# Where layer 0's output product lets the modulation tiles run: the last eight weight tiles without any, the first twenty-four with more

## The chip, the cores and the metric

The kernel runs on one core of one Trainium2 chip. The metric is the time of one execution on the device in microseconds (us). A core has the engines PE (TensorE, matmuls), DVE (VectorE), ACT (ScalarE), POOL (GpSimd) and SP (SyncE, which here issues nearly all loads). Each takes its instructions strictly in its own order and waits on semaphores for the others.

## The reference, cut to what matters

Two pairs of transformer layers on a sequence of 256 tokens with 2048 channels, float32. The first pair (layers 0 and 1) is modulated: three vectors per layer come from one product of the 2048-element condition with a 2048 x 6144 matrix.

```python
def first_block(x, c, positions, w_ada, b_ada, w_in, ..., w_out, ln_g, ln_b):
    c_act = jax.nn.silu(c)
    for l in range(DEPTH):                       # DEPTH = 2
        mod = c_act @ w_ada[l] + b_ada[l]
        shift, scale, gate = jnp.split(mod, 3, axis=-1)
        h = _layernorm(x) * (1.0 + scale[:, None, :]) + shift[:, None, :]
        p = h @ w_in[l]
        ...
        y = jnp.concatenate([y_f, y_a], axis=-1) @ w_out[l]
        x = _layernorm(DEEPNORM_ALPHA * x + gate[:, None, :] * y, ln_g[l], ln_b[l])
    return x
```

The second pair (`even_layer`, `odd_layer`) is of the same kind without modulation. Nothing that is computed changes here; layer 1's shift and scale only have to be there when layer 1 begins.

## The kernel before, in words

Every instruction comes from one plan (`Plan.whole`). It first writes a list of jobs, one for each tile of weights (128 partitions x 1024 numbers, 512 KB), and `run` then walks this list and appends steps to an order that all engines follow, each taking its own part.

A **weight tile** (job mode `split`) goes through five stations: SP loads it into one of nine staging buffers `stg` (line 1406), ACT writes its rounded high part into one of four buffers `whi` (line 1893), DVE writes the rest into `wlo` (line 2214), PE multiplies three times with high and low parts of the activations (`Hh`, `Hl`; line 1506), and the end of PE's work frees the staging buffer. A **modulation tile** (mode `ada`) needs PE only at the very end: SP loads it into one of the same nine buffers, and DVE multiplies it with the condition and adds it into the accumulator `AC` (line 2127, the first of sixteen is a plain product on line 2223). That frees the buffer. Buffers are handed out strictly in the order in which the plan frees them.

`run` prepares a weight tile (load, ACT part, DVE part) three weight tiles ahead of its matmuls (`AHEAD = 3`). A modulation tile puts its DVE instruction in at the place where it stands in the list.

Layer 0's output product (`w_out(0, "w_out0")`) has 32 weight tiles: four groups of eight, a group for each 512 output columns. I call them t0 to t31. Each takes 12 matmuls of 512 columns. After a group DVE runs the "out" block: six instructions on 128x512 (lines 2377, 2127, 2382, twice) that apply the gate, add to X and take statistics. At the head of the product two things of the previous stage are late: the last gate of y (four instructions on line 2127, `Z` and `TMP`) and the split of y into `Hh` and `Hl` (`y_split`, line 2368: four pieces for t2 to t5, then two for t6 and t7). The order of these around the tiles is fixed by the plan, and every one of them stands in DVE's single row.

When t31 is done the layer's closing part follows (`post_norm`, a chain on DVE, PE and ACT), then layer 1 begins with `lead`.

`interleave(n0, extra, n1, some)` takes the list's jobs from `n0` on (the body, here 84 weight tiles: 52 of layer 0's other products, then the 32 of `w_out0`) and deals the modulation tiles (`extra`, 98 jobs) in between: 76 of them evenly beside the first `n1` = 52, the other 22 evenly beside the rest.

Of the kernel before, what the change touches and what calls it, by code (L numbers as in the profile page):

```python
# [61 lines left out]
class Plan:  # L62
# [991 lines left out]

    def interleave(self, n0, extra, n1, some):
        body = self.jobs[n0:]
        del self.jobs[n0:]
        out, e = [], 0  # L1060
        for i, j in enumerate(body):
            due = some * (i + 1) / n1 if i < n1 else some + (len(extra) - some) * (i + 1 - n1) / (len(body) - n1)
            while e < len(extra) and e < due:
                out.append(extra[e])
                e += 1
            out.append(j)
        out += extra[e:]
        self.jobs.extend(out)

    def lead(self, first, trans, layer, columns=None):  # L1070

# [24 lines left out]
    def whole(self):  # L1096
        self.banks.get()
        self.banks.put(0, ("ca", 1))
        begin0 = self.mla(0)
        first, rest = self.jobs[0:24], self.jobs[24:]  # L1100
        del self.jobs[:]
        self.ln(("x_landed", 32))
        self.normed(range(4))
        ada = [self.ada_pe(q) for q in range(8)]

        def setup_bias():
            b, fr = self.banks.get()
            self.step("bias", bank=b, free=fr)
            self.banks.put(b, self.tick("bias"))

        def table(kind, out, by=1):
            b, fr = self.now(self.banks)
            self.step(kind, bank=b, free=fr)
            self.banks.put(b, self.tick(out, by))

        def turn(n):
            self.step("turn", n=n)
            if n == 1:
                self.ar = (("scr_landed", 32), ("rope_tab", 2))
                begin0()  # L1120

        tables = [lambda: table("gains", "vec"), lambda: table("biases", "buckets", 2), lambda: table("angles", "angle"),
                  lambda: turn(0), lambda: turn(1)]
        self.jobs.extend(ada[0][0])

        def cols(q):
            ada[q][1]()

        def enter(q):
            self.mod_h(0, (q,))  # L1130
            if q == 7:
                self.zw = self.h[KT - 1]

        def enter0():
            cols(0)
            enter(0)

        def pair(q, n):
            if q < 8:
                self.jobs.extend(ada[q][0][2 * n:2 * n + 2])  # L1140

        self.jobs[4]["pre"] = setup_bias
        self.jobs[6]["pre"] = enter0
        for q in range(8):
            j0, j1, j2 = (first[8 * g + q] for g in range(3))
            j0["last_chunk"] = q == 7
            self.jobs.append(j0)
            if q == 0:
                pair(1, 0)
                pair(1, 1)  # L1150
                self.jobs.append(j1)
                pair(1, 2)
                pair(1, 3)
                self.jobs.append(j2)
                j2["after"] = lambda: cols(1)
                self.jobs.append(ada[2][0][0])
                ada[2][0][0]["pre"] = lambda: enter(1)
                self.jobs.append(ada[2][0][1])
                pair(2, 1)
                continue  # L1160
            pair(q + 1, 2)
            pair(q + 1, 3)
            self.jobs.append(j1)
            if q < 7:
                j1["after"] = lambda q=q: cols(q + 1)
                if q < 6:
                    ada[q + 2][0][0]["pre"] = lambda q=q: enter(q + 1)
                else:
                    j2["pre"] = lambda: enter(7)
            pair(q + 2, 0)  # L1170
            self.jobs.append(j2)
            if q < 6:
                j2["after"] = tables[q - 1]
            pair(q + 2, 1)

        n0 = len(self.jobs)
        self.jobs.extend(rest)
        self.w_out(0, "w_out0")
        ex = []
        for c0 in (2 * D, 2 * D + 1024):  # L1180
            ex += self.ada(0, c0, 1024)
        for c0 in (0, 1024, D, D + 1024):
            ex += self.ada(1, c0, 1024)
        self.interleave(n0, ex, 52, 76)

        def norm1():
            p = self.post_norm(0)
            self.ln(p["out"][1], p)

        def scale():  # L1190
            for fin in self.scale_sums:
                fin()

        n1 = self.lead(norm1, lambda qs: self.mod_h(1, qs), lambda: self.mla(1), scale)
        self.w_out(1, "w_out1")
        ex = []
        for c0 in (2 * D, 2 * D + 1024):
            ex += self.ada(1, c0, 1024)
        self.interleave(n1 + 6, ex, 70, 32)

        def norm2():
            p = self.post_norm(1)
            self.rms(p["squared"], p["ss"], 8)

        self.lead(norm2, lambda qs: self.transposed("en", None, qs), self.even)
        self.w_out(2, "even_w_out")

        def norm3():
            self.ar = (self.mm_last,)
            self.h_free = self.mm_last  # L1210
            self.rms(self.x[1, 3], None, 8)

        self.lead(norm3, lambda qs: self.transposed("on", None, qs), self.odd)
        self.w_out(3, "odd_w_out")
        self.run()
        self.drain()
        return self
# [36 lines left out]
def build(nc, A):  # L1254
    with ExitStack() as ctx:
# [28 lines left out]
        for whole, tiles in ((AR, stg), (ARL, wlo)):  # L1284
            tiles += [whole[:, 3072 + i * 1024:4096 + i * 1024].rearrange("p (k n) -> p k n", k=2) for i in range(EXTRA)]
# [98 lines left out]
        def sync(e):  # L1384
            q = Queue(e)
            e.dma_start(ROWS[0:16, :], A["c"].rearrange("a (k p) -> (a k) p", p=128)).then_inc(SEM["c_landed"], 16)
            e.dma_start(IDN[:, :], cst[:, 0:128]).then_inc(SEM["c_landed"], 16)
            for t in range(2):
                e.dma_start(X[:, t, :], A["x"][0, t * 128:(t + 1) * 128, :]).then_inc(SEM["x_landed"], 16)
            for kind, s in plan.order:  # L1390
                if kind == "load":
                    slot = s["slot"]
                    q.wait_all(s["free"])
                    w, rows, n = tile_shape(s["src"])
                    whole = stg[slot][:, :, :].rearrange("p k n -> p (k n)")
                    if w == "b_ada":
                        (_, _, _, l, c0), = s["src"]
                        e.dma_start(whole[0:1, :], A["b_ada"][l:l + 1, c0:c0 + n]).then_inc(SEM[f"landed{slot}"], 16)
                        continue
                    if rows * n == 1024:  # L1400
                        dst, pat = whole, [[1024, 128], [1, 1024]]
                    else:
                        dst, pat = stg[slot][:, :, 0:n], [[rows * n, 128], [n, rows], [1, n]]
                    src = bass.AP(A[w].tensor, tile_at[w], pat)
                    tile_at[w] += 128 * rows * n
                    e.dma_start(dst, src).then_inc(SEM[f"landed{slot}"], 16)
                elif kind == "out" and s["l"] == 3 and s["g"] == 3:
                    t = s["t"]
                    q.wait_ge(s["done"])
                    e.dma_start(A["out"][0, t * 128:(t + 1) * 128, 1536:2048], X[:, t, 1536:2048]).then_inc(SEM["out_last"], 16)  # L1410
            q.wait_ge(("out_landed", 96))
            q.wait_ge(("out_last", 32))
            q.wait_ge(("scr_landed", 32))
# [1301 lines left out]
```

## Time and profile before

| | us |
|---|---|
| median of 3 runs | 1558.52 |
| lowest and highest of them | 1557.95, 1561.76 |
| the profiled execution | 1556.26 |
| its span | 1554.4 |
| what lies around the span | 1.86 |
| PE busy in the span | 1486.9 |
| DVE busy in the span | 1065.7 |

The page gives PE as busy for 96% of the span and DVE for 69%. These are shares over the whole execution, of stages with different limits. The output product of layer 0 lies between 345 and 433 us of the span, and only that stretch and its surroundings are touched by the change. In the views below a start is given in us from the span's start; "idle before" in square brackets is the time for which the engine stood before this instruction, and who released it. An instruction on DVE is reported longer than the distance to the next start, since neighbours overlap by a little: distances between starts are what DVE's row costs.

### The profile page before, as it was taken

The numbers are of one execution on the slowest core, as the hardware profiler recorded it, in microseconds if no ns is written. First come the engines' busy times: TensorE is split into PE (matmuls) and PEld (weight loads), VectorE is DVE, ScalarE is ACT, GpSimd is POOL, SyncE is SP. The second block draws the span as 40 slices with busy tenths as digits, with TensorE's granted clock in tenths as the row PEclk, the third lists the DMA queues.
The fourth block names the chain that finished last, engine by engine and source line by source line (L and its number), as shares of the span: only waits on it lengthen the run. The fifth ranks groups of instructions, "written<-read, shape, count | busy, mean of one in ns | idle before, by whom it ended". The sixth has DMA issues, their size and how long they took to land.

```text
span 1554.4 us, 25460 instructions
## 1 busy us (share of the span) xinstructions
PE 1486.9 (96%) x10123; PEld 1316.1 (85%) x10123; DVE 1065.7 (69%) x1732; ACT 706.8 (45%) x1218; POOL 45.3 (3%) x66
## 2 busy tenths in 40 slices
PE   5999999989979999999979999999998999999999
PEld 3778789988869788998859997799987998889987
DVE  3348689899987667577575684875655667775653
ACT  2235234344345445444335444654444546665442
POOL 3000000000000000000000000010000000000000
PEclk9999999999989999999999999999999999999999
DMA  9999889998837556776745555466665554445673
GB/s 357 406 406 330 283 294 364 348 365 338 329 90 266 191 195 207 251 247 205 217 148 179 177 169 151 123 219 187 184 196 163 151 162 121 124 123 160 183 223 98
DMA packets 102126, 347.15 MB, mean 223 GB/s; under 512 B 11392, under 2 KB 21876, under 8 KB 101240
## 3 DMA queue, kind: packets, MB, share of 16 engines
q1 hardware_dynamic: 96888, 327.42, 62.7%
q0 software_dynamic: 5120, 18.11, 3.5%
q8 instruction: 80, 1.31, 0.3%
q14 instruction: 38, 0.31, 0.1%
HBM read 343.27 MB, written 2.21 MB: 222 GB/s over the span
## 4 chain that ended last, share of the span: by engine, by line
PE 78%; DVE 11%; issue 4%; DMA 4%; ACT 3%; SPq 0%; DVEq 0%; ACTq 0%
PE PM L1506 66%; PE PB L1506 8%; DVE wlo L2214 2%; DMA stg<-in_w_in 2%; DVE AC L2127 2%; ACT whi L1893 1%; DVE X L2127 1%; DMA stg<-in_w_ada 1%; ACT AR L1893 1%; PE PB L1741 1%; PE PB L1713 1%; PE PB L1816 1%; DVE SM L2127 0%; PE PB L1788 0%; ACT Hh L1893 0%
## 5 line engine op out<-in xcount | busy, mean ns | idle before, releaser
L2214 DVE TENSOR_TENSOR wlo<-stg,whi 128x1024 fp32r<-128x1024 f32 (+2 forms) x417 | 497.9, 1203 | 324.5 <-ACT whi L1893 322.2
L1893 ACT ACTIVATE whi<-stg 128x1024 fp32r<-128x1024 f32 (+2 forms) x417 | 430.3, 1038 | 455.2 <-PE PM L1506 348.5
L1506 PE MATMUL PM<-Hh,whi 128*128 128x256 f32 x1824 | 526.2, 291 | 11.5 <-DVE wlo L2214 7.6
L1506 PE MATMUL PM<-Hh,wlo 128*128 128x256 f32 x1776 | 500.3, 285 | 0.0
L1506 PE MATMUL PM<-Hl,whi 128*128 128x256 f32 x1824 | 497.7, 284 | 0.0
L1506 PEld LDWEIGHTS PM<-Hh,whi 128*128 128x128 f32 x1824 | 352.4, 193 | 29.5 <-issue 17.0
L1506 PEld LDWEIGHTS PM<-Hh,wlo 128*128 128x128 f32 x1776 | 343.6, 193 | 0.0
L1506 PEld LDWEIGHTS PM<-Hl,whi 128*128 128x128 f32 x1824 | 342.5, 193 | 0.4
L1506 PE MATMUL PM<-whi,Hh 128*128 128x512 f32 (+1 forms) x576 | 223.3, 389 | 0.4 <-DVE wlo L2214 0.4
L1506 PE MATMUL PM<-wlo,Hh 128*128 128x512 f32 (+1 forms) x576 | 220.1, 383 | 0.0
L1506 PE MATMUL PM<-whi,Hl 128*128 128x512 f32 (+1 forms) x576 | 218.3, 384 | 0.0
L2127 DVE SCALAR_TENSOR_TENSOR AC<-stg,CA,AC 128x1024 f32<-128x1024 f32 x120 | 153.6, 1280 | 6.6 <-DMA stg<-in_w_ada 4.0
L1506 PEld LDWEIGHTS PM<-whi,Hh 128*128 128x128 f32 x576 | 108.3, 188 | 23.4 <-issue 1.5
L1506 PEld LDWEIGHTS PM<-wlo,Hh 128*128 128x128 f32 x576 | 108.3, 188 | 21.0 <-issue 0.2
L1506 PEld LDWEIGHTS PM<-whi,Hl 128*128 128x128 f32 x576 | 107.1, 188 | 21.4
L1506 PE MATMUL PM<-whi,ARL 128*128 128x512 f32 (+1 forms) x272 | 86.1, 383 | 0.0
L1893 ACT ACTIVATE AR<-PB 128x384 f32<-128x384 f32 (+2 forms) x110 | 47.3, 471 | 75.4 <-PE PB L1506 28.0
L1506 PE MATMUL PB<-AR 64*128 64x256 f32 (+4 forms) x576 | 71.1, 353 | 3.5 <-ACT AR L1893 2.2
L1506 PEld LDWEIGHTS PB<-AR 64*128 64x128 f32 (+2 forms) x576 | 46.2, 170 | 21.2 <-issue 6.0
L1506 PEld LDWEIGHTS PM<-whi,ARL 128*128 128x128 f32 x272 | 51.1, 188 | 10.3 <-issue 0.4
L1506 PE MATMUL PM<-wlo,ARL 128*128 128x512 f32 (+1 forms) x144 | 54.4, 378 | 0.0
L1893 ACT ACTIVATE AR<-PM 128x256 f32<-128x256 f32 (+2 forms) x58 | 24.1, 466 | 57.1 <-PE PM L1506 57.1
(287 smaller groups left out, 1389.5 us busy)
## 6 DMA issues: line engine op xcount, KB each, us to landing
stg<-in_w_ada SPq DMA_DIRECT2D x163, 512.0 KB, 6.2
stg<-in_w_in SPq DMA_DIRECT2D x105, 512.0 KB, 5.4
stg<-in_even_w_in SPq DMA_DIRECT2D x80, 512.0 KB, 3.6
stg<-in_odd_w_in SPq DMA_DIRECT2D x72, 512.0 KB, 3.6
stg<-in_w_out SPq DMA_DIRECT2D x64, 512.0 KB, 4.5
stg<-in_even_w_out SPq DMA_DIRECT2D x32, 512.0 KB, 3.6
stg<-in_odd_w_out SPq DMA_DIRECT2D x32, 512.0 KB, 3.5
AR<-in_w_ada SPq DMA_DIRECT2D x29, 512.0 KB, 14.5
```

Source lines behind the costliest of these rows:

```text
L1506: return e.matmul(out, l, r, start=start, stop=stop, skip_group_check=True)
L1713: ins = e.transpose(B[:, kk * S + t * 128:kk * S + t * 128 + 128], XN[:, t, k * 128:(k + 1) * 128], IDN[:, :])
L1741: ins = e.matmul(B[:, 0:S], ar(UU + t * 1024 + s["g"] * 128, 128), CSS[:, t, :], start=t == 0, stop=t == 1)
L1816: ins = e.transpose(B[:, n * 128:(n + 1) * 128], L[:, n * 128:(n + 1) * 128], IDN[:, :])
L1893: return e.activation(out, x, f, **k)
L2127: return e.scalar_tensor_tensor(out=out, in0=in0, scalar=scalar, in1=in1, op0=op0, op1=op1)
L2214: e.tensor_tensor(wlo[s["slot"]][:, :, 0:n], stg[s["slot"]][:, :, 0:n], whi[s["hi"]][:, :, 0:n].bitcast(F32), ALU.subtract).then_inc(SEM[" ...
```

## The change

`interleave` gets a fifth argument, `bare`: the number of weight tiles at the body's end that get no extra job beside them. The call for layer 0 passes 8.

```diff
-    def interleave(self, n0, extra, n1, some):
-        body = self.jobs[n0:]
+    def interleave(self, n0, extra, n1, some, bare=0):
+        end = len(self.jobs) - bare
+        body, last = self.jobs[n0:end], self.jobs[end:]
         del self.jobs[n0:]
         out, e = [], 0
         for i, j in enumerate(body):
...
         out += extra[e:]
-        self.jobs.extend(out)
+        self.jobs.extend(out + last)
...
-        self.interleave(n0, ex, 52, 76)
+        self.interleave(n0, ex, 52, 76, 8)
```

The first 52 weight tiles keep their 76 jobs, since `n1` and `some` are the same. The last 22 modulation tiles, which stood beside 32 weight tiles, now stand beside 24. PE's, ACT's and POOL's orders of instructions are the same as before; DVE's and SP's are not. In the rows below every line number of the kernel after is one higher, because one line was added.

DVE, from the four pieces of `Hl` for t2 to t5 on. `AC<-stg` is a modulation tile, `wlo<-stg` the low part of a weight tile (here t3 to t6), `TMP<-TMP,PM` and `Z` the last gate. Before:

```order
L2368 TENSOR_TENSOR Hl<-Z,Hh 128x512 x4
L2214 TENSOR_TENSOR wlo4<-stg4,whi3 128x1024
L2127 SCALAR_TENSOR_TENSOR AC<-stg0,CA,AC 128x1024
L2214 TENSOR_TENSOR wlo5<-stg5,whi0 128x1024
L2127 SCALAR_TENSOR_TENSOR AC<-stg1,CA,AC 128x1024
L2214 TENSOR_TENSOR wlo7<-stg7,whi1 128x1024
L2214 TENSOR_TENSOR wlo3<-stg3,whi2 128x1024
L2127 SCALAR_TENSOR_TENSOR TMP0<-TMP0,PM0 128x512
L2127 SCALAR_TENSOR_TENSOR Z<-TMP0,Z 128x512
```

The same place after the change:

```order
L2369 TENSOR_TENSOR Hl<-Z,Hh 128x512 x4
L2128 SCALAR_TENSOR_TENSOR AC<-stg4,CA,AC 128x1024
L2215 TENSOR_TENSOR wlo0<-stg0,whi3 128x1024
L2128 SCALAR_TENSOR_TENSOR AC<-stg5,CA,AC 128x1024
L2215 TENSOR_TENSOR wlo1<-stg1,whi0 128x1024
L2128 SCALAR_TENSOR_TENSOR AC<-stg7,CA,AC 128x1024
L2215 TENSOR_TENSOR wlo3<-stg3,whi1 128x1024
L2224 TENSOR_SCALAR AC<-stg4,CA 128x1024
L2215 TENSOR_TENSOR wlo2<-stg2,whi2 128x1024
L2128 SCALAR_TENSOR_TENSOR TMP0<-TMP0,PM0 128x512
L2128 SCALAR_TENSOR_TENSOR Z<-TMP0,Z 128x512
```

The last gate now has four modulation tiles ahead of it since `Hl` x4, where it had two.

DVE from the first "out" block on (its last row is the one on `STA`). Before, the weight tiles are t11 to t15:

```order
L2382 BN_STATS STA<-X 128x6
L2127 SCALAR_TENSOR_TENSOR AC<-stg5,CA,AC 128x1024
L2214 TENSOR_TENSOR wlo6<-stg6,whi3 128x1024
L2214 TENSOR_TENSOR wlo7<-stg7,whi0 128x1024
L2127 SCALAR_TENSOR_TENSOR AC<-stg3,CA,AC 128x1024
L2214 TENSOR_TENSOR wlo4<-stg4,whi1 128x1024
L2127 SCALAR_TENSOR_TENSOR AC<-stg0,CA,AC 128x1024
L2214 TENSOR_TENSOR wlo5<-stg5,whi2 128x1024
L2214 TENSOR_TENSOR wlo1<-stg1,whi3 128x1024
```

After the change:

```order
L2383 BN_STATS STA<-X 128x6
L2215 TENSOR_TENSOR wlo7<-stg7,whi3 128x1024
L2128 SCALAR_TENSOR_TENSOR AC<-stg3,CA,AC 128x1024
L2215 TENSOR_TENSOR wlo4<-stg4,whi0 128x1024
L2128 SCALAR_TENSOR_TENSOR AC<-stg2,CA,AC 128x1024
L2215 TENSOR_TENSOR wlo5<-stg5,whi1 128x1024
L2128 SCALAR_TENSOR_TENSOR AC<-stg6,CA,AC 128x1024
L2215 TENSOR_TENSOR wlo8<-stg8,whi2 128x1024
L2128 SCALAR_TENSOR_TENSOR AC<-stg3,CA,AC 128x1024
```

Modulation and weight tiles now alternate strictly: to the second "out" block they are seven beside eight, where they were six beside eight.

DVE from the last modulation tile to the next "out" block, after the change (t22 to t26):

```order
L2128 SCALAR_TENSOR_TENSOR AC<-stg2,CA,AC 128x1024
L2215 TENSOR_TENSOR wlo1<-stg1,whi2 128x1024
L2215 TENSOR_TENSOR wlo6<-stg6,whi3 128x1024
L2215 TENSOR_TENSOR wlo7<-stg7,whi0 128x1024
L2215 TENSOR_TENSOR wlo3<-stg3,whi1 128x1024
L2215 TENSOR_TENSOR wlo4<-stg4,whi2 128x1024
L2378 TENSOR_TENSOR TMP0<-PM2,GT 128x512
L2128 SCALAR_TENSOR_TENSOR X<-X,TMP0 128x512
```

From t22 to t31 there is nothing on DVE but weight tiles and the "out" blocks; six modulation tiles stood there before.

## Rows read from the trace of the kernel before

**Rows 1.** The page's first line, and busy time by engine.

```profile
span 1554.4 us, 25460 instructions
PE 1486.9 (96%) x10123; PEld 1316.1 (85%) x10123; DVE 1065.7 (69%) x1732; ACT 706.8 (45%) x1218; POOL 45.3 (3%) x66
```

**Rows 2.** Busy time by stretch: columns in the second line.

```profile
core 0: us, PE busy (x) PEld busy (x) DVE busy (x) ACT busy (x) POOL busy (x), PEclk, DMA share, GB/s
333.00:345.00 12.00, 12.00 (x103) 12.00 (x101) 11.34 (x10) 5.24 (x5) 0.00 (x0) 1.00 1.02 411
345.00:375.50 30.50, 30.13 (x134) 24.59 (x132) 30.05 (x35) 16.51 (x20) 0.00 (x0) 1.00 0.87 326
375.50:411.00 35.50, 35.46 (x156) 29.40 (x157) 33.29 (x31) 13.81 (x13) 0.00 (x0) 1.00 0.92 357
411.00:433.00 22.00, 21.95 (x97) 17.84 (x95) 17.94 (x21) 7.43 (x7) 0.00 (x0) 1.00 0.78 286
455.00:475.00 20.00, 18.55 (x155) 18.37 (x155) 16.66 (x23) 14.10 (x21) 0.00 (x0) 0.99 0.44 130
```

**Rows 3.** Waits of 345 to 433 us: waiter, releaser, us, times, longest.

```profile
DVE wlo L2214 <- ACT whi L1893: 4.6, 5, 1.5
PE PM L1506 <- DVE wlo L2214: 0.4, 1, 0.4
```

**Rows 4.** The chain that ended last, between 373 and 434 us: start, us, what.

```profile
374.35 1.15 DVE wlo L2214
...
375.54 57.43 PE PM L1506 x252
...
432.99 0.70 DVE TMP L2377
```

**Rows 5.** DVE in order of time, from t3's low part to t11's.

```profile
350.40 1.22 DVE L2214 TENSOR_TENSOR wlo<-stg,whi 128x1024 fp32r<-128x1024 f32 x1
351.54 1.28 DVE L2127 SCALAR_TENSOR_TENSOR AC<-stg,CA,AC 128x1024 f32<-128x1024 f32 x1
352.73 1.22 DVE L2214 TENSOR_TENSOR wlo<-stg,whi 128x1024 fp32r<-128x1024 f32 x1
...
359.99 1.47 DVE L2368 TENSOR_TENSOR Hl<-Z,Hh 128x512 fp32r<-128x512 f32 x2
...
363.71 0.75 DVE L2223 TENSOR_SCALAR AC<-stg,CA 128x1024 f32<-128x1024 f32 x1
364.38 2.36 DVE L2214 TENSOR_TENSOR wlo<-stg,whi 128x1024 fp32r<-128x1024 f32 x2
...
374.27 2.35 DVE L2214 TENSOR_TENSOR wlo<-stg,whi 128x1024 fp32r<-128x1024 f32 x2
```

**Rows 6.** DVE further on: low parts of t16, t17, t18 and t19.

```profile
384.01 1.23 DVE L2214 TENSOR_TENSOR wlo<-stg,whi 128x1024 fp32r<-128x1024 f32 x1 [0.40 <-ACT whi L1893]
...
386.54 1.23 DVE L2214 TENSOR_TENSOR wlo<-stg,whi 128x1024 fp32r<-128x1024 f32 x1
...
389.10 1.23 DVE L2214 TENSOR_TENSOR wlo<-stg,whi 128x1024 fp32r<-128x1024 f32 x1
...
394.35 1.21 DVE L2214 TENSOR_TENSOR wlo<-stg,whi 128x1024 fp32r<-128x1024 f32 x1
```

**Rows 7.** PE in order of time: the first matmul of t0 and of t2.

```profile
345.00 0.40 PE L1506 MATMUL PM<-whi,ARL 128*128 128x512 f32 x1
...
350.46 0.39 PE L1506 MATMUL PM<-whi,Hh 128*128 128x512 f32 x1
```

**Rows 8.** PE after two waits, one long and one short.

```profile
329.01 0.40 PE L1506 MATMUL PM<-Hh,whi 128*128 128x256 f32 x1 [3.52 <-DVE wlo L2214]
...
332.76 0.28 PE L1506 MATMUL PM<-Hh,whi 128*128 128x256 f32 x1
332.88 0.28 PE L1506 MATMUL PM<-Hl,whi 128*128 128x256 f32 x1
...
462.25 0.63 PE L1713 MATMUL PB<-IDN,Z 128*128 128x128 f32 x4 [1.46 <-DVE Z L2333]
```

## The prediction, made before the changed kernel had run

> **What bounds the kernel now.** Three views in this order. The page first [rows 1]: PE is busy for 96% of the span, so the default is that only what makes PE wait or stop waiting counts, and DVE's 69% seems to leave room. Next the stretches [rows 2], because that 69% is an average. In layer 0's output product DVE is busy for 30.05 of 30.5 us, then 33.29 of 35.5, and only in the last third 17.94 of 22.0; the DMA engines run at 0.87, 0.92 and 0.78 of their time. PE is busy nearly throughout. So for two thirds of this stage PE, DVE and DMA are close to a tie, and the slack of DVE lies in the last third, exactly where the change removes work from it. Third, who waits for whom: over the whole product PE waits once, 0.4 us for a low part [rows 3]. The chain shows where: DVE's low part of t11, and from then 252 matmuls (21 tiles) in 57.43 us without a break until t31 ends at 432.97, when the closing part starts at once [rows 4]. After 375.54 the stage is PE's alone.
>
> **PE's pace and DVE's price list.** 57.43 / 21 is 2.73 us for a tile. t0 begins at 345.00 and t2 at 350.46 [rows 7], the same 2.73. So PE reaches t6 at 350.46 + 4 x 2.73 = 361.4, t11 at 375.54, and t19 at 375.54 + 8 x 2.73 = 397.4. On DVE, distances between starts [rows 5]: a low part 351.54 - 350.40 = 1.14 us, a modulation tile 352.73 - 351.54 = 1.19 (1.2 below), the plain product that opens an accumulator 364.38 - 363.71 = 0.67.
>
> **What the change removes.** Six modulation tiles leave the ten last weight tiles, some 6 x 1.2 = 7.2 us of DVE time. Their place from t22 on is beside PE work that does not wait [rows 3, 4], so I cost the removal at nothing: what hides them is the unbroken run of matmuls. It would be worth something only if PE waited there, and the closing part starts with PE's last matmul in either order.
>
> **What it adds.** The same instructions, earlier. Since DVE runs without a gap from 350.40 to beyond 382, each one put ahead of a needed result makes it later by its full price. DVE's order up to `Hl` x4 is unchanged, so 350.40, where that ends, is a fixed point [rows 5]. Three results decide:
>
> - The last `Hl` pieces, for t6 and t7. Before them now stand three modulation tiles and the plain product, where two tiles stood: + 1.2 + 0.67 = 1.9 us. The first piece began at 359.99 [rows 5] and takes 0.7 (1.47 for the two), so it ends at 362.6 instead of 360.7. PE arrives at 361.4: PE waits 1.2 us. t7's low part, two more places back, adds 0.4.
> - t11. By then seven modulation tiles and the plain product have run, where it was five: + 2.4 us. t11's low part was ready at 375.49 and PE took it at 375.54 [rows 4]; it now starts at 377.9. PE is late by 2.4 in total, of which the first item is part, not an addition.
> - t19, the first tile behind the second "out" block. Counted from 350.40, fifteen modulation tiles against ten: + 5 x 1.2 = 6.0 us. Its low part ended at 394.35 + 1.21 = 395.56 [rows 6], so now 401.6; PE would be there at 397.4. Late by 4.2 us in total.
>
> From t22 on DVE has only 1.14 us of work for a tile besides the "out" blocks, against PE's 2.73, so nothing later is late: what is lost by t19 stays lost, and nothing grows. The sum is **+ 4.2 us**.
>
> One term in it is a choice. Before t16 DVE stood 0.40 us for a high part; t17 and t18 follow at distances of 2.53 and 2.56 us [rows 6], where a modulation tile and a low part cost 1.2 + 1.14 = 2.34: two more gaps of 0.2. These come from loads. If the added DVE work filled all three, the total would be 4.2 - 0.8 = 3.4. The other end: all eight pairs between t11 and t19 at the distance of 2.53 add 8 x 0.2 = 1.6, less the 0.4 that is in the figures already: 5.4. I keep 4.2, since the loads are no fewer and their share was 0.92 there [rows 2]; a gap that a load makes does not go away by adding loads.
>
> **Loads.** SP issues the same number, in another order. Two loads for a tile cost at the highest rate of the table, 411 GB/s [rows 2], 2 x 0.524 MB / 411 = 2.55 us, under PE's 2.73. So the loads fit, with little over. In an "out" block DVE frees no staging buffer for 4.1 us (t18 to t19 less one low part, 394.35 - 389.10 - 1.14 [rows 6]), and SP stands behind it with all loads that follow; this is the danger of the dense part, and the second rival.
>
> **ACT, POOL, accumulators.** ACT's order is the same; it splits when a load is there and when PE has freed one of four `whi`, and its busy time is about half [rows 2]. POOL has nothing here. The two scale accumulators are read only when layer 1 begins; they are complete earlier, which nobody waits for.
>
> **Against which time.** The profiled execution took 1556.26 us, the median of the runs is 1558.52. The sum is made on the former, 1556.26 + 4.2 = 1560.5, and I carry the difference to the median: 1558.5 + 4.2 = 1562.7. It is 0.27% of the time. About 0.3%, 4.7 us, is what a measurement of this kernel can tell from no change.
>
> **The rivals.**
>
> *Absorbed.* PE does not lose what the count says, because the lead of DVE over PE is larger than one trace shows. For it: t9, the second of the two low parts at 364.38 [rows 5], is done at 366.7, and PE comes at 350.46 + 7 x 2.73 = 369.6, 2.9 us later. Against: t7's low part is done at 363.8, when DVE goes on to the plain product, and PE comes at 364.1; t11 has no lead at all; and the delays are counted to just those. It would give 0 to + 2: 1559.5.
>
> *Loads become the bound.* SP waits through the "out" block, DMA falls idle, and afterwards weight tiles come late at 1.28 us a load. If 3 of the 4.1 us of each of the two dense "out" blocks are lost to DMA, fifteen loads and 3 us take 15 x 1.28 + 3 = 22.2 us against PE's 21.8, beside DVE's own 8 x 2.34 + 4.1 = 22.8; when the two do not overlap well, 1 to 2 us come on top in each of two periods: + 6 to + 8, 1565.5. The profile would show DVE waiting for high parts, and these for loads, between 378 and 400.
>
> *The clock.* After a PE wait of 3.52 us matmuls took 0.40 us where others of this shape take 0.28; the 19th starts at 332.76, 3.75 us later, where 18 distances of 0.12 would be 2.16 [rows 8]: 1.6 us lost at the lower (1.2 GHz) of the clock's two levels. After a wait of 1.46 us [rows 8] the granted clock of that stretch stayed at 0.99 [rows 2]. The new waits are 1.2, 0.4, 0.8 and up to 1.8 us, most like the second row, so I price this at nothing. If two of them do cost it: 4.2 + 3.2, 1566.
> The Trainium skill, "TensorE: Matmul & The Clock Gate", section "A second HAM failure mode: psum-queue depth-cycling", tells of short idles between groups of matmuls that come often enough to let the clock fall and rise again. By that rule this rival would happen; the row of the short wait speaks against it, and no stretch here has several such waits in a row.
>
> *Faster.* Place: the start of layer 1, where PE waits 1.46 us at 462.25 [rows 8] for an instruction of DVE that stands behind three low parts of layer 1's first tiles. With the last eight tiles bare their loads go out earlier. If that wait is in truth one for loads, and if PE is not delayed before t19 at all, the change gains up to 1.5 us: 1557. It decides only if both hold; the DVE row there waits for ACT, not for DMA, and ACT's order is unchanged.
>
> **How the numbers follow.** Forecast (3.4 to 5.4 late): 0.60, of which a third above 4.7. Absorbed 0.14. Loads 0.13. Clock 0.07. Faster 0.06, of which 0.04 is left for a gain over 0.3% by something that I do not see. Slower by over 0.3%: 0.20 + 0.13 + 0.07 = 0.40. Faster: 0.04. Within: 0.56. The range starts at 1559.0, which cuts off the faster case and about a third of the absorbed one, and ends at 1566.0, which takes in the loads and half of the clock: about 0.15 is left out.
>
> **What the profile after would show.** Right: PE waits for DVE three or four times between 360 and 401 us, the first at t6 for `Hl` (about 1.2 us), then at t11 and t19 for low parts, 4 us in all; from t19 on no wait; t31 ends near 437 instead of 432.97; DVE's busy share 411 to 433 falls below 0.7; all after the product is the same, shifted. Wrong: t31 ends within 1 us of 433 (absorbed); DVE waits of over 1 us for high parts before t19 (loads); a granted clock under 0.97 between 360 and 410 (clock); a change of over 1 us in the part after t31 would be a cause that I have not counted.

## The result, and the profile after

| | before | changed | ratio (95% interval) |
|---|---|---|---|
| median of 6 and 6 runs | 1559.79 us (1557.95 to 1562.3) | 1569.16 us (1566.55 to 1573.79) | 1.0058 (1.0044 to 1.0073) |
| profiled execution | 1556.26 us, span 1554.4 | 1567.74 us, span 1565.9 | |

The change makes the kernel slower by 9.4 us. The forecast was 4.2 us slower, 1562.7; the result is above its range. Measured twice more beside the experiments, the change cost 4.9 and 6.9 us. The forecast had the sign, and its size is below all three.

Busy times did not move [rows 1]:

```profile
span 1565.9 us, 25460 instructions
PE 1489.6 (95%) x10123; PEld 1317.0 (84%) x10123; DVE 1067.5 (68%) x1732; ACT 707.2 (45%) x1218; POOL 45.4 (3%) x66
```

The stretches of the product (same columns as [rows 2]; t0 starts at 346.88 here, 1.9 us later than before):

```profile
core 0: us, PE busy (x) PEld busy (x) DVE busy (x) ACT busy (x) POOL busy (x), PEclk, DMA share, GB/s
345.00:375.50 30.50, 27.94 (x129) 22.49 (x128) 29.36 (x31) 15.61 (x19) 0.00 (x0) 1.00 0.89 336
375.50:411.00 35.50, 32.42 (x135) 25.99 (x134) 34.20 (x35) 11.81 (x13) 0.00 (x0) 0.95 0.91 332
411.00:443.00 32.00, 31.86 (x141) 26.06 (x139) 20.97 (x23) 11.60 (x11) 0.00 (x0) 1.00 0.72 243
```

PE now idles some 2.5 and 3 us in the first two stretches and not in the third; in the second the granted clock is 0.95, where it was 1.00. The waits of 345 to 440 us, against [rows 3], which end at 433:

```profile
DVE wlo L2215 <- ACT whi L1894: 10.9, 10, 1.5
PE PM L1507 <- DVE wlo L2215: 3.4, 3, 2.1
PE PM L1507 <- DVE Hl L2369: 2.2, 1, 2.2
```

PE waits four times for DVE, 5.6 us, instead of once for 0.4; and DVE itself waits ten times for high parts where it was five times. Of the ten only three stand before t19 (0.73, 0.48 and 0.28 us), of the five one (0.40); the others come when DVE is ahead of PE and cost nothing. PE in order of time shows the four waits (in brackets) and what follows the last:

```profile
346.88 0.40 PE L1507 MATMUL PM<-whi,ARL 128*128 128x512 f32 x1
...
355.59 0.50 PE L1507 MATMUL PM<-whi,Hh 128*128 128x512 f32 x1 [0.36 <-DVE wlo L2215]
...
366.22 0.47 PE L1507 MATMUL PM<-whi,Hh 128*128 128x512 f32 x1 [2.17 <-DVE Hl L2369]
366.52 0.39 PE L1507 MATMUL PM<-wlo,Hh 128*128 128x512 f32 x1
...
381.46 0.50 PE L1507 MATMUL PM<-whi,Hh 128*128 128x512 f32 x1 [1.00 <-DVE wlo L2215]
...
405.60 0.58 PE L1507 MATMUL PM<-whi,Hh 128*128 128x512 f32 x1 [2.08 <-DVE wlo L2215]
405.97 0.63 PE L1507 MATMUL PM<-wlo,Hh 128*128 128x512 f32 x1
406.40 0.63 PE L1507 MATMUL PM<-whi,Hl 128*128 128x512 f32 x1
...
409.35 0.39 PE L1507 MATMUL PM<-whi,Hh 128*128 128x512 f32 x1
```

They stand at t3, at t6 (the last `Hl` pieces), t11 and t19. After the wait at t6 the matmuls take the usual 0.39 us. After the one at t19 seven matmuls in a row take 0.6 us, 0.43 us apart instead of 0.23: the lower, 1.2 GHz level of the clock. The chain that ended last, against [rows 4]:

```profile
404.40 1.15 DVE wlo L2215
405.55 0.04 issue
405.60 37.28 PE PM L1507 x156
442.87 0.02 issue
442.89 0.70 DVE TMP L2378
```

The unbroken run of matmuls begins at t19 instead of t11. Its 156 matmuls would take 57.43 x 156 / 252 = 35.55 us at the pace of [rows 4]; they take 37.28, so the matmuls at the lower clock cost 1.7 us. The product from t0's first matmul to the end of t31 is 442.86 - 346.88 = 95.98 us, before 432.96 - 345.00 = 87.96: **8.0 us longer** (the chain, added up from rounded pieces, ends 0.01 us later). Two pieces of the 11.5 us between the two spans lie outside the product: 1.9 us had come before t0, and 1.6 us come at 510 to 530 us, where a granted clock of 0.91 stands against 1.00. The first is spread between executions; whether the second belongs to the change is taken up at experiment 3.

### The profile page after: what moved, and what is told of

It reads as the page before. It is cut to its first block, busy times and chain, and to the rows that moved or that the text cites. A ratio compares the mean times of both kernels' runs of the same rounds, so it can differ in the third digit from the quotient of the medians.

```text
span 1565.9 us, 25460 instructions
## 1 busy us (share of the span) xinstructions
PE 1489.6 (95%) x10123; PEld 1317.0 (84%) x10123; DVE 1067.5 (68%) x1732; ACT 707.2 (45%) x1218; POOL 45.4 (3%) x66
## 3 DMA queue, kind: packets, MB, share of 16 engines
q8 instruction: 80, 1.31, 0.3%
## 4 chain that ended last, share of the span: by engine, by line
PE 76%; DVE 10%; DMA 6%; issue 3%; ACT 3%; SPq 1%; DVEq 0%; ACTq 0%
PE PM L1507 64%; PE PB L1507 8%; DMA stg<-in_w_in 4%; DVE wlo L2215 2%; DVE AC L2128 2%; ACT whi L1894 1%; SPq L1407 1%; DVE X L2128 1%; DMA stg<-in_w_out 1%; PE PB L1742 1%; ACT AR L1894 1%; PE PB L1817 1%; PE PB L1714 1%; DVE SM L2128 0%; PE PB L1789 0%
```

## The experiments

Two causes were to be told apart: the count, that is, DVE instructions put ahead of results that PE waits for; and the order of the loads, in which modulation loads now stand ahead of weight loads. "Product" is t0's first matmul to the end of t31 in the profiled execution. Where a run is named "a" it starts from the changed kernel, "b" from the kernel before. Each time is given with the median of the kernel before in the same session.

**1. Short DVE work.** The 22 modulation tiles of the product (from the 77th on) are loaded whole but multiplied over 64 columns only. The rest of their product is left out.

```diff
+        for j in ex[76:]:
+            j["small"] = True
...
+                        m = 64 if s["small"] else s["n"]
+                        acc, w = acc_of(s, i)[:, 0:m], staged(s, i)[:, 0:m]
```

> The kernel before, but the DVE instruction of the 22 modulation tiles beside layer 0's output product works on 64 of 1024 columns; they are loaded in full (layer 1's shift and scale are not what they should be, all else runs as it is). DVE theory (the modulation tiles' time in DVE's row is what makes PE wait): PE's one wait at t11 of 0.4 us goes, -0.5 to -1 us against before. Load theory (loads and staging buffers pace the stage): the same time as before, within 1 us.

> The changed kernel with the same shortening of the 22 DVE instructions to 64 columns, full loads (layer 1's shift and scale are left incomplete). DVE theory: no wait of PE of over 0.5 us between t0 and t31 and no fall of the clock there; within 1 us of the shortened kernel before, 9 us under the changed kernel. Load theory: PE still waits at t6, t11 and t19, behind high parts that wait for loads, and the time is 4 to 9 us above the shortened kernel before.

Measured: b 1559.46 against 1560.69, ratio 0.9995 (0.9984 to 1.0007); a 1559.93, 1.0001 (0.999 to 1.0012). Product: b 87.24 with no PE wait; a 89.10 with one. DVE and PE of a:

```profile
356.03 1.22 DVE L2217 TENSOR_TENSOR wlo<-stg,whi 128x1024 fp32r<-128x1024 f32 x1 [1.08 <-ACT whi L1896]
357.17 0.25 DVE L2228 TENSOR_SCALAR AC<-stg,CA 128x64 f32<-128x64 f32 x1
...
359.15 1.23 DVE L2217 TENSOR_TENSOR wlo<-stg,whi 128x1024 fp32r<-128x1024 f32 x1 [1.73 <-ACT whi L1896]
```

```profile
363.77 0.47 PE L1509 MATMUL PM<-whi,Hh 128*128 128x512 f32 x1 [1.59 <-DVE Hl L2373]
```

The modulation tile now costs DVE 0.25 us instead of 1.2, and still PE waits 1.59 us at t6, since DVE stands 1.08 and 1.73 us for high parts just before. With DVE made light, t11 and t19 are in time. So the order of the loads alone can make PE wait at t6, and in this kernel only there. It is worth 89.10 - 87.24 = 1.9 us of product, of which some may be the later entry that is told of below; the medians of a and b differ by 0.5 us, too little to tell from nothing. The time went as the DVE theory had it, the wait at t6 as the load theory had it. A heavy DVE can hide such a delay, since it reaches the high part later, so this does not show that loads cost as much in the changed kernel itself.

**2. Short loads.** The same tiles keep their DVE work, but of each only 64 columns are loaded; the multiplication takes another operand in SBUF, so these sums are not the reference's.

```diff
+                    if s["small"]:
+                        dst, pat = whole[:, 0:64], [[1024, 128], [1, 64]]
...
+                        if s["small"]:
+                            q.wait_ge(("gate_row", 32))
+                            w = GT[:, 0:1024]
```

> The kernel before, but of the same 22 modulation tiles only 64 of 1024 columns are loaded, and their DVE instruction, full in length, reads other data (layer 1's shift and scale are left incomplete). DVE theory: as before, 0 to -1 us. Load theory: -1 to -2 us, since DVE's waits for high parts go.

> The changed kernel with the same 22 loads cut to 64 columns and full DVE instructions (layer 1's shift and scale are left incomplete). DVE theory: PE still waits at t6, t11 and t19; 3 to 7 us above the kernel before with cut loads, the more the clock falls; DVE's own waits for high parts (1.5 us before t19 in the changed kernel) are gone. Load theory: within 1 us of the kernel before with cut loads.

Measured: b 1559.79 against 1560.69, 1.0004 (0.999 to 1.0018); a 1561.70, 1.0008 (0.9999 to 1.0018). Product: b 88.02, a 90.36. The stretches of a and its waits:

```profile
346.10:376.60 30.50, 30.27 (x133) 24.45 (x132) 30.20 (x34) 14.69 (x19) 0.00 (x0) 1.00 0.65 200
376.60:412.00 35.40, 33.68 (x148) 27.25 (x147) 32.82 (x32) 13.08 (x13) 0.00 (x0) 1.00 0.63 205
```

```profile
PE PM L1511 <- DVE wlo L2219: 1.7, 2, 1.0
PE PM L1511 <- DVE Hl L2377: 0.2, 1, 0.2
```

With DMA at 0.65 of its time instead of 0.9 the waits at t11 and t19 remain: 1.03 and 0.69 us. This is DVE's count alone. Product + 2.3 us, medians + 1.9 us, both below the 3 to 7 that were expected. But a entered the product 1.0 us better than b (entry 2.02 against 3.05, below); an estimate at equal entry is 2.3 + 1.0 = 3.3 us, close to the forecast's lower end of 3.4. In these two experiments the loads show at t6 and the count at t11 and t19, and neither was followed by slow matmuls. Apart they lengthen the product by 1.9 and 2.3 us, together by 8.0. Of the 3.8 us that are left over 1.7 are the slow matmuls. The other 2.1 appear only where both act; that the count has used up the lead that hid the loads would explain them, but no run shows it by itself.

**3. How much two executions differ.** The kernel before, run once more as a kernel of its own, and the changed kernel twice more.

> The kernel before, once more, for a second trace. Both theories: 0 us. Open is where its stages lie: whether the 1.9 us by which the changed kernel entered the output product later, and the clock's fall after it, are spread between executions (then this trace shows shifts of 1 to 2 us too) or belong to the change (then it lies within 0.3 us of the first trace at 345 us).

> The changed kernel once more, for a second trace. The account of the first trace (5 DVE instructions more ahead of t19, 6.0 us; a DVE row that entered the product 0.8 us later against PE; 1.5 us of DVE waits for loads; a clock that fell at t19, 1.8 us) expects the product from t0 to the end of t31 to take 94 to 96 us where the entry and the clock are the same, 93 to 94 if Hl x4 starts 3.0 us after t0, and 1.8 less if the clock holds. The time: +8 to +10 us. Rival (a part of the 9 us lies outside the product and belongs to the change): the product takes 92 and the time is still +9.

> The changed kernel a third time, since the first two measurements stand at +9.4 and +4.9 us against the kernel before, with intervals that touch nowhere. If the size of the effect depends on how late DVE enters the output product against PE (2.0 to 4.6 us between Hl x4 and t0 in the traces so far) and on whether the clock falls at t19, it lies between the two, +5 to +8 us, and the trace's product takes 87.5 us plus its waits plus 1.8 for a fall of the clock. If one of the two was a disturbed measurement, it falls on the other.

Measured: the kernel before 1559.65 against 1559.98, 0.9993 (0.9982 to 1.0003). The changed kernel 1566.28 against 1561.37, 1.0030 (1.0021 to 1.0040), and 1566.53 against 1559.67, 1.0049 (1.0037 to 1.0062). In the traces:

| trace | t0 at | entry | PE waits in the product | product | after t31 |
|---|---|---|---|---|---|
| before | 345.00 | 2.99 | 0.41 | 87.96 | 1121.4 |
| before, again | 347.68 | 2.41 | none | 87.37 | 1123.0 |
| changed | 346.88 | 3.83 | 0.36, 2.17, 1.00, 2.08 | 95.98 | 1123.0 |
| changed, again | 346.01 | 4.59 | 1.04, 1.31, 1.04, 2.13 | 95.96 | 1123.0 |
| changed, third | 345.35 | 3.81 | 0.34, 1.31, 1.00, 2.91 | 96.09 | 1122.9 |

"Entry" is the start of `Hl` x4 on DVE less t0's first matmul on PE: how late DVE is, against PE, when the product begins. The product's length repeats to 0.13 us in the changed kernel and to 0.6 in the kernel before, although the single waits do not repeat. The place of t0 does not repeat either. The 1.6 us at the lower clock after t31 stand in the second trace of the kernel before as well, so they can come without the change. They are in all three traces of the changed kernel, though, and over all experiments in five of the six traces with the last eight weight tiles bare and in two of the eight others, so a part of the change in them is not excluded. What the change does for certain is the 8.0 us of the product. All three traces have the slow matmuls at t19; the second:

```profile
404.72 0.61 PE L1507 MATMUL PM<-whi,Hh 128*128 128x512 f32 x1 [2.13 <-DVE wlo L2215]
405.13 0.63 PE L1507 MATMUL PM<-wlo,Hh 128*128 128x512 f32 x1
```

Three measurements give + 9.4, + 4.9 and + 6.9; three products give + 8.0 to + 8.1 against the first trace of the kernel before and + 8.6 to + 8.7 against the second. The second measurement lies outside the + 8 to + 10 that were expected, while its product is as expected. Why the medians differ from each other and from the product was not found.

**4. The removal alone.** From the kernel before, five of the last six modulation tiles are left out; the very last moves up to the place of the first of them, and all others keep their places (`total` keeps the dealing as for 98). Their part of the scale is left out.

```diff
+        del ex[92:97]
-        self.interleave(n0, ex, 52, 76)
+        self.interleave(n0, ex, 52, 76, total=98)
```

> The kernel before without five of the six modulation tiles in the last eight weight tiles' reach: they are left out with their loads, nothing is added elsewhere (layer 1's scale is incomplete). My theory: taking them away is worth nothing, 0 us within 1; t31 ends 87.9 us after t0 begins, as before. Rival (the last tiles are held back by them): -1 to -3 us.

Measured: 1559.32 against 1559.98, 0.9997 (0.9984 to 1.001); product 88.36, one wait of 0.49 us. Some 6 us of DVE work and five loads of 0.5 MB taken away beside a PE that does not wait are worth nothing.

**5. Half of the change.** Four bare tiles at the end instead of eight.

```diff
-        self.interleave(n0, ex, 52, 76, 8)
+        self.interleave(n0, ex, 52, 76, 4)
```

> The change with four bare tiles instead of eight: the 22 modulation tiles stand beside 28. DVE theory: by t19 two to three modulation tiles more than before instead of five, so PE is 2.4 to 3.6 us late where the full change made it 6.3; +2 to +4 us, +5 if the clock falls. Rival (only strict alternation with loads hurts): no less than +7, or nothing.

Measured: 1560.73 against 1559.98, 1.0011 (0.9997 to 1.0024), which cannot be told from nothing and is under the expected + 2 to + 4; product 89.77, + 2.4 against the second trace of the kernel before and + 1.8 against the first. Its waits:

```profile
PE PM L1507 <- DVE wlo L2215: 0.8, 1, 0.8
PE PM L1507 <- DVE Hl L2369: 0.6, 1, 0.6
```

No wait above 1 us and no slow matmuls. Half of the change costs 0.8 us by the runs and some 2 by the trace, less than half of the whole. This fits the count: the first tiles eat DVE's lead, and only what is beyond the lead costs.

**6. The product's head as before.** Changed kernel, but t0 to t7 get the six modulation tiles they had; the dense part begins at t8. `deal` takes pairs of weight tiles and modulation tiles and spreads the second evenly over the first.

```diff
-        self.interleave(n0, ex, 52, 76, 8)
+        self.deal(n0, ex, ((52, 76), (8, 6), (16, 16), (8, 0)))
...
+    def deal(self, n0, extra, parts):
+        body, e, start = self.jobs[n0:], 0, 0
+        del self.jobs[n0:]
+        for tiles, jobs in parts:
+            for i in range(tiles):
+                while e < len(extra) and e < start + jobs * (i + 1) / tiles:
+                    self.jobs.append(extra[e])
+                    e += 1
+                self.jobs.append(body.pop(0))
+            start += jobs
```

> Last eight tiles bare, but the first eight keep the six modulation tiles that they had; the other sixteen go one to one beside t8 to t23. If what counts is the number of modulation tiles ahead of t19 in DVE's row (four more than before instead of five), PE does not wait for Hl at t6, but waits more at t11 and t19, and the total is that of the change less 1.2 us: +7 to +8.5 us. If the waits add up one by one and the one at t6 is a cost of its own (2.2 us in the trace), the total is that of the change less 2.5 to 3.5: +5.5 to +7 us.

Measured: 1565.47 against 1559.98, 1.0033 (1.0021 to 1.0045); product 92.89. The wait at t6 is gone, the others are there:

```profile
PE PM L1518 <- DVE wlo L2226: 3.1, 2, 1.9
```

1.18 us at t11, 1.90 at t19 and seven slow matmuls after it. By its number, + 5.5 us, this is the second alternative of the expectation, waits that add up one by one. The traces say otherwise. The product is 3.1 us shorter than the changed kernel's 95.98: entry is better by 1.27 us (2.56 against 3.83), and DVE takes 51.76 us from `Hl` x4 to t19's low part instead of 53.61, 1.2 of it for one modulation tile fewer and 0.65 for shorter waits for high parts. At t19 PE takes the low part as soon as it is done, so DVE's total lateness there is what PE pays, in whatever pieces. The expectation's "less 1.2" had left the entry and the loads out.

**7. The other way: modulation tiles later.** If DVE has slack in the last third and none before, the tiles belong there. `late` gives the layer's weight tiles 44 to 51, the eight ahead of t0, 9 modulation tiles instead of 12, t0 to t7 5, and the last sixteen 14; the product holds 25 instead of 22. `early_late` has 6 in each of the later eights, and puts the surplus beside the layer's first 16 weight tiles, 27 instead of 23.

```diff
-        self.interleave(n0, ex, 52, 76)
+        self.deal(n0, ex, ((44, 64), (8, 9), (8, 5), (8, 6), (8, 7), (8, 7)))
```

```diff
-        self.interleave(n0, ex, 52, 76)
+        self.deal(n0, ex, ((16, 27), (28, 39), (8, 9), (8, 5), (8, 6), (8, 6), (8, 6)))
```

> The opposite of the change. Three of the 76 modulation tiles beside the 52 earlier weight tiles are taken from the last eight of these (nine there instead of twelve), and all 25 beside the output product are dealt 5, 6, 7 and 7 to its four groups, so that DVE has fewest where PE has waited and most where PE has lead. DVE-count theory: the wait of 3.5 to 4.1 us some 16 us before t0 shrinks by 2 x 1.2 us, with it perhaps the half clock behind it (1.6 us); no wait in the product: -2.4 to -4.5 us against before. Rival (the wait before the product is one for loads, or 7 tiles beside the last groups are too many): 0 to +3 us.

> The dealing of the run named late, mended by its trace: there PE waited 1.8 us at t28, with a fall of the clock, since 25 modulation tiles beside the output product were too many. Here 23, dealt 5, 6, 6 and 6; nine beside the last eight earlier tiles as there; the other two go to the first sixteen of the earlier tiles (27 instead of 23.4), where DVE is busy for 17.6 of 30 us and DMA at 0.81 between 160 and 190 us. Count theory: the gain before the product stays (t0 some 5 us earlier than before), the product takes 88 us: -3.5 to -6 us against before. Rival (the early tiles are as tight as the late ones): -1 to -3 us, or a new wait between 130 and 240 us.

Measured: `late` 1558.68 against 1561.37, 0.9980 (0.9968 to 0.9992), 2.7 us faster. `early_late` 1554.45 against 1559.67, 0.9967 (0.9954 to 0.9980), **5.2 us faster, better than both kernels**. The gain is not in the product, which is longer in both. Some 15 us before t0 every trace of the old order has a PE wait of 3.4 to 4.1 us with slow matmuls after it, and these two kernels shorten it. PE there in the second trace of the kernel before, in `late` and in `early_late`:

```profile
330.49 0.58 PE L1506 MATMUL PM<-Hh,whi 128*128 128x256 f32 x1 [4.13 <-DVE wlo L2214]
```

```profile
324.98 0.39 PE L1518 MATMUL PM<-Hh,whi 128*128 128x256 f32 x1 [2.00 <-DVE wlo L2226]
```

```profile
331.55 0.39 PE L1518 MATMUL PM<-Hh,whi 128*128 128x256 f32 x1 [1.31 <-DVE wlo L2226]
```

`late` reaches t0 at 339.48, 5.5 us earlier than the first trace of the kernel before, and loses most of it again: its product is 92.36 us long, with a wait of 1.83 us at t27 (60 matmuls, five tiles, before the end) and seven slow matmuls after it, behind an "out" block with seven modulation tiles beside eight weight tiles. `early_late` has six there: no wait above 0.7 us in the product, 89.24 us, at the price of a fuller DVE in the layer's first half. At 160 to 190 us, the kernel before and `early_late`:

```profile
160.00:190.00 30.00, 28.24 (x140) 23.34 (x138) 17.55 (x21) 6.53 (x16) 2.96 (x2) 1.00 0.81 277
```

```profile
160.00:190.00 30.00, 28.13 (x137) 22.91 (x136) 21.63 (x28) 6.56 (x15) 2.85 (x2) 1.00 0.85 303
```

4 us more of DVE in 30, and PE's busy time the same. Not everywhere is the early work free, though. At 135 us two modulation tiles now stand in a row on DVE where the kernel named `late` has one, and PE waits 2.10 us for what ACT makes out of DVE's next results, where it waits 0.65 to 1.08 in `late` and the two traces of the kernel before:

```profile
135.07 2.66 DVE L2139 SCALAR_TENSOR_TENSOR AC<-stg,CA,AC 128x1024 f32<-128x1024 f32 x2
```

```profile
140.31 1.21 PE L1732 MATMUL PB<-AR,ROT 128*128 128x256 f32 x2 [2.10 <-ACT AR L1905]
```

```profile
130.00:160.00 30.00, 27.70 (x138) 24.24 (x139) 24.21 (x42) 11.28 (x21) 0.00 (x0) 0.83 0.73 260
```

The granted clock is 0.83 there, against 1.00 and 0.94 in the traces of the kernel before. With this the trace of `early_late` reaches t0 at 346.05, no earlier than the kernel before, and its product is longer than before too. It is the trace of the slowest of the five executions (1558.55). So the 5.2 us stand by the runs alone: that they come from the shorter wait ahead of t0 is likely, since `late` shows it, but no trace of `early_late` shows it.

## Why the prediction came out too low

**Which engine, where, and which way: right.** DVE sets the first two thirds, PE the last third [rows 2]. The removal is worth nothing (experiment 4). The waits came at the three places named, t6, t11 and t19, with a small fourth at t3, and after t19 there is none; DVE's share from 411 on fell to 20.97 / 32 = 0.66, below 0.7.

**The term that was counted is right.** From t0, t19's low part started 394.35 - 345.00 = 49.35 us later before, and 57.44 after:

```profile
404.32 1.22 DVE L2215 TENSOR_TENSOR wlo<-stg,whi 128x1024 fp32r<-128x1024 f32 x1
```

The 8.1 us between are 6.0 for five modulation tiles, as counted, and 2.1 that the sum did not have. Less the lead of 1.8 us that the count gave to DVE, the count alone makes 4.2; experiment 2 gives 2.3 for it as measured, 3.3 as an estimate at equal entry. The 2.1 us are the next two steps together. Their sum repeats, 2.09, 2.08 and 2.17 us in the three traces of the changed kernel against the first of the kernel before, but its division does not.

**First failed step: "DVE's order up to `Hl` x4 is unchanged, so 350.40 is a fixed point".** Against DVE's clock it is fixed, against PE's it isn't: entry was 2.99 us before and 3.83 after: + 0.84. Three traces of the changed kernel have 3.8 to 4.6, those of the kernel before 2.4 and 3.0. The other runs say that this is probably of the change, by way of the loads. Of the traces with the old order ahead of t0 and full loads, those with a modulation load moved in ahead of t3's weight load have 3.81, 4.59, 3.81, 3.86 and 3.60 (changed three times, short DVE work, half change); those without have 2.99, 2.41, 2.72, 3.40 and 2.56 (before twice, short DVE work, removal, head as before). With short loads it is 2.02 for the changed order. What in the loads does it was not followed up.

**Second failed step: "the loads are no fewer", so their gaps stay as they are.** The forecast kept the gaps of [rows 6] and added none. From the start of `Hl` x4 to t19's low part DVE took 394.35 - 347.99 = 46.36 us before and 404.32 - 350.71 = 53.61 after: 7.25 more, of which 6.0 are the count and 1.25 longer gaps for high parts (by the same sum 0.48 and 1.35 in the other two traces). In the first trace the largest new one stands before `Hl`, on DVE:

```profile
350.71 2.49 DVE L2369 TENSOR_TENSOR Hl<-Z,Hh 128x512 fp32r<-128x512 f32 x4
353.12 1.28 DVE L2128 SCALAR_TENSOR_TENSOR AC<-stg,CA,AC 128x1024 f32<-128x1024 f32 x1
...
360.12 0.75 DVE L2224 TENSOR_SCALAR AC<-stg,CA 128x1024 f32<-128x1024 f32 x1
...
361.59 1.23 DVE L2215 TENSOR_TENSOR wlo<-stg,whi 128x1024 fp32r<-128x1024 f32 x1 [0.73 <-ACT whi L1894]
...
365.39 1.47 DVE L2369 TENSOR_TENSOR Hl<-Z,Hh 128x512 fp32r<-128x512 f32 x2
```

on the queue of SP:

```profile
354.43 0.33 SPq L1407 DMA_DIRECT2D stg<-in_w_ada  x1
354.80 1.40 SPq L1407 DMA_DIRECT2D stg<-in_w_out  x1
```

and on ACT:

```profile
360.50 1.06 ACT L1894 ACTIVATE whi<-stg 128x1024 fp32r<-128x1024 f32 x1 [3.37 <-DMA stg<-in_w_out]
```

Staging buffers are handed out in the order of the loads. The `Hl` x4 of 2.4 us frees none; the modulation load at 354.43 goes when the modulation tile begun at 353.12 has freed its buffer, and t6's weight load stands behind it. It is issued at 354.80, and ACT starts on it at 360.50, 5.7 us later; DVE waits 0.73 us. In the kernel before that weight load was issued ahead of `Hl` x4, at 346.73, together with t5's. The prediction looked for this danger at the "out" blocks, where it stayed small in this trace (0.48 us at 390.08, 0.28 at 392.79), and added up rates: two loads in 2.55 us fit into 2.73. What it left out is that a load's place in the row also decides when it is there. With the later entry this made 2.17 us at t6 out of the forecast 1.2.

It does not happen in every execution. In the other two traces of the changed kernel DVE reaches t6 without a gap, here the second, and PE waits 1.31 us there, close to the forecast:

```profile
360.00 0.75 DVE L2224 TENSOR_SCALAR AC<-stg,CA 128x1024 f32<-128x1024 f32 x1
360.67 1.22 DVE L2215 TENSOR_TENSOR wlo<-stg,whi 128x1024 fp32r<-128x1024 f32 x1
```

Their gaps lie later, up to 1.08 us at t16 in the third. So the loads cost something in each trace, but where, and how much beside the entry, changes.

**Third failed step: the clock, priced at nothing.** The forecast waits were 0.4 to 1.8 us, so the row of the 1.46 us wait was taken as nearest [rows 8]. With entry and loads the wait at t19 was 2.08, 2.13 and 2.91 us, and slow matmuls follow it in all three traces: + 1.7 us. So the rival "clock" was a part of the truth, as a follow-up of the other two. Its sign, a granted clock under 0.97 between 360 and 410, was drawn too wide to see it: the clock is 0.97 there in all three traces. The rule of the Trainium skill, "TensorE: Matmul & The Clock Gate", section "A second HAM failure mode: psum-queue depth-cycling", tells of short idles between groups of matmuls that come often enough to let the clock fall and rise. The traces agree in that waits far shorter than the 3.52 us of [rows 8] stand before the fall. Each of them was the last of two to four waits 10 to 25 us apart, so whether one is enough is not shown.

**The sum with measured terms**: 4.2 + 0.84 + 1.25 + 1.7 = 8.0 us of product, as the first trace has. t31's end, forecast for 437, is 442.87, of which 1.9 are the later t0. The median adds 1.4 us to the 8.0, and in the other two measurements takes 1.1 and 3.1 away; this is not explained. The 1.6 us after t31 are one of the signs of a wrong forecast that the prediction named, "a cause that I have not counted": it is there, and whether it is the change's stays open.

**The chances.** The forecast was called "within 0.3%" because 4.2 us lay 0.5 us under that bound. The loads and the clock, priced at nothing, could only add, and the entry was taken from one trace, where it could have come out either way. A sum with open terms of mostly one sign belongs above its own bound, not below it.

## What to carry to other kernels

Work of a second engine that stands beside a bound engine without slack costs its full price less the lead, and pays nothing where it is taken from a stretch with slack. So move it from where the waits are to where they are not, and stop before the target itself is full: by the runs 2.7 us were gained by moving it later and 5.2 by moving some of it also much earlier. Look for a new wait at the place it goes to. Where staging buffers are handed out in order, follow each moved load through its queue: look at which free buffer it waits for and which load stands behind it, especially across a long instruction that frees none. And when several small terms are set to nothing, look at their signs and at whether one brings on the next, as lateness here made a wait long enough to cost the clock too.

## What the runs showed of the hardware

- Waits of PE of about 2 us, in matmuls that otherwise follow each other, can be followed by the lower clock. In the product, seven matmuls at 0.6 us each and 0.43 us apart followed waits of 1.83, 1.90, 2.08, 2.13 and 2.91 us, a loss of 1.7 us each time; none followed waits of 1.59, 1.31, 1.18 us and less. One wait of 2.17 us (t6 in the changed kernel) and one of 2.00 us (before t0 in `late`) were not followed by any, so length alone does not decide it. What else does stays open.
- Executions of one program differ by more than their medians show: the same order reached t0 between 345.0 and 350.2 us, the two kernels with the order changed ahead of it left out of this, and one stretch of lower clock at about 510 us, worth 1.6 us, is there in one trace of the kernel before and not in the other. In the changed kernel and in the first trace of the kernel before:

```profile
509.90:529.90 20.00, 20.00 (x93) 16.47 (x92) 16.50 (x35) 8.91 (x14) 0.00 (x0) 0.91 0.57 189
```

```profile
500.00:520.00 20.00, 20.00 (x100) 16.66 (x99) 18.01 (x36) 9.68 (x15) 0.00 (x0) 1.00 0.61 201
```

PE is busy for all of 20 us in both, with 93 matmuls in the one and 100 in the other.

- The clock also falls where PE does not wait. Just before the seven slow matmuls of that stretch PE runs 24 matmuls of a single column, which count as busy:

```profile
511.65 2.73 PE L1507 MATMUL PB<-ONE,AR 128*128 128x1 f32 x24
```

All 14 traces have these matmuls at that place; in seven of them slow matmuls follow, in the other seven none.
